# Asking for the next expert's rows late in the turn instead of early

## What is computed

```python
def _moe_swiglu(x, w_router, w_gate, w_up, w_down):
    ...
    logits = (xf @ w_router).astype(jnp.float32)
    top_logit, top_idx = lax.top_k(logits, TOP_K)        # 8 experts, 2 per token
    top_w = jax.nn.softmax(top_logit, axis=-1)
    ...
    def expert_block(args):
        xs, e = args
        return (jax.nn.silu(xs @ w_gate[e]) * (xs @ w_up[e])) @ w_down[e]
    ...
    out = jnp.zeros_like(xf).at[row_token].add(y_rows)   # weighted rows, added at their token
```

## Time and profile before

| | |
|---|---|
| median of three runs | 2572.55 us |
| the profiled execution: its time, its span | 2571.28 us, 2569.5 us |
| PE (TensorE matmuls) busy | 2514.3 us, 98% |
| DVE (VectorE) busy | 1837.9 us, 72% |
| ACT (ScalarE) busy | 1302.9 us, 51% |
| POOL (GpSimd) busy | 125.7 us, 5% |
| granted TensorE clock, mean | 0.993 |
| HBM over the span | 219 GB/s |

### The profile page before, as it was taken

One profiled execution on the slowest core, in us unless ns is written; L12 is line 12 of the kernel. 1 busy time (PEld: TensorE's weight loads), 2 busy tenths in 40 slices (PEclk: granted clock), 3 DMA queues, 4 the chain that ended last, 5 costly groups with the idle time before them and its releaser, 6 DMA issues.

```text
span 2569.5 us, 41311 instructions
## 1 busy us (share of the span) xinstructions
PE 2514.3 (98%) x16342; PEld 2169.7 (84%) x16342; DVE 1837.9 (72%) x2266; ACT 1302.9 (51%) x1535; POOL 125.7 (5%) x136
## 2 busy tenths in 40 slices
PE   8999999999999999999999999999999999999997
PEld 7888999878899988789998887888888888888886
DVE  6657777855777555365555643689899899899898
ACT  5454545553544431224334212267677677777775
POOL 1100000300000001200000111000000000000000
PEclk9999999999999999999999999999999999999999
DMA  5344553423544431136554321399999999999995
GB/s 213 131 181 155 188 196 133 147 99 131 213 179 183 148 131 67 67 131 237 183 178 148 116 68 66 128 377 366 357 370 360 363 367 356 364 368 354 363 369 225
DMA packets 78909, 563.96 MB, mean 219 GB/s; under 512 B 8880, under 2 KB 9136, under 8 KB 11440
## 3 DMA queue, kind: packets, MB, share of 16 engines
q1 hardware_dynamic: 76320, 550.93, 57.2%
q0 software_dynamic: 2448, 11.01, 1.1%
HBM read 559.81 MB, written 2.10 MB: 219 GB/s over the span
## 4 chain that ended last, share of the span: by engine, by line
PE 91%; DVE 4%; ACT 3%; issue 2%; DMA 0%; DVEq 0%; ACTq 0%; SPq 0%; POOL 0%
PE bank L655 24%; PE bank L1141 18%; PE bank L1166 10%; PE bank L645 10%; PE bank L684 7%; PE bank L716 4%; PE bank L736 3%; PE bank L669 2%; DVE w_lo L2503 1%; PE bank L1151 1%; PE bank L963 1%; PE bank L977 1%; PE bank L974 1%; ACT w_hi L1659 1%; PE bank L810 1%
## 5 line engine op out<-in xcount | busy, mean ns | idle before, releaser
L2503 DVE TENSOR_TENSOR w_lo<-ring,w_hi 128x2048 fp32r<-128x2048 f32 x216 | 486.0, 2288 | 46.8 <-ACT w_hi L1659 46.8
L1659 ACT ACTIVATE w_hi<-ring 128x2048 fp32r<-128x2048 f32 x216 | 405.0, 1917 | 20.2 <-PE bank L1141 16.7
L1141 PE MATMUL bank<-w_hi,xe_hi 128*128 128x512 f32 x792 | 312.0, 394 | 1.1
L1141 PE MATMUL bank<-w_lo,xe_hi 128*128 128x512 f32 x792 | 308.8, 390 | 0.0
L1141 PE MATMUL bank<-w_hi,xe_lo 128*128 128x512 f32 x792 | 308.2, 389 | 0.0
L655 PE MATMUL bank<-x_hi,w_hi 128*128 128x256 f32 x1008 | 285.3, 283 | 0.0
L655 PE MATMUL bank<-x_hi,w_lo 128*128 128x256 f32 x1008 | 285.2, 283 | 0.0
L655 PE MATMUL bank<-x_lo,w_hi 128*128 128x256 f32 x1008 | 285.2, 283 | 0.0
L1754 DVE TENSOR_TENSOR w_lo<-ring,w_hi 128x2048 fp32r<-128x2048 f32 x97 | 222.1, 2290 | 86.1 <-ACT w_hi L1280 84.0
L645 PE MATMUL bank<-xT,ring 128*128 128x256 f32 x1088 | 253.8, 385 | 1.1 <-ACT Z L1568 1.1
L1280 ACT ACTIVATE w_hi<-ring 128x2048 fp32r<-128x2048 f32 x99 | 189.4, 1914 | 109.2 <-PE bank L684 71.4
(11 more groups left out here) (378 smaller groups left out, 5093.1 us busy)
## 6 DMA issues: line engine op xcount, KB each, us to landing
ring<-in_stream SPq DMA_DIRECT2D x431, 1024.0 KB, 5.1
yT<-in_stream SPq DMA_DIRECT2D x54, 1024.0 KB, 6.9
xT<-in_stream SPq DMA_DIRECT2D x27, 1024.0 KB, 7.2
Z<-in_stream SPq DMA_DIRECT2D x8, 1024.0 KB, 8.3
norm_rows<-in_rows POOLq DMA_DIRECT2D x4, 1024.0 KB, 7.7
par<-in_par SPq DMA_DIRECT2D x1, 1335.0 KB, 9.7
cst<-in_cst SPq DMA_DIRECT2D x1, 1216.0 KB, 13.6
xres<-in_x SPq DMA_DIRECT2D x2, 512.0 KB, 4.5
```

What stands on the lines that cost most here:

```text
L1141: r = mm(banks[4 + j % 2], a[:, k, :], moe_part(b, i)[:, q * 512:(q + 1) * 512], start=(k == 0 and a is xe_hi and b is w_hi), stop=(k == K ...
L1659: act_(moe_part(w_hi, at), moe_slot(at), ACT.Copy).then_inc(*A.done("moe_hi", at))
L2503: v.tensor_tensor(moe_part(w_lo, at), moe_slot(at), moe_part(w_hi, at).bitcast(F32), ALU.subtract)\
```

## The change

The one-hot matrix for the next turn is made at j = 7 behind that for `pickw` instead of at j = 2. TensorE multiplies it with the token numbers at j = 8, right behind the transposes of `pickw`, instead of at j = 4. VectorE copies `row_at` at j = 9, ahead of `pickT`, instead of at j = 5, and behind the waits for `slot_weight` and the scatter. GpSimd's code is the same; it issues the gather when the copy is done. TensorE's wait for `row_at` ahead of the transposes at j = 8 is gone. No instruction other than that wait is added or removed.

```diff
@@ TensorE, in turn()
                         if j == 8:
-                            pe.wait_ge(*V.of("row_at"))
                             pe.wait_ge(*V.of("pickw"))
                             for tb in range(TB):
                                 r = nc.tensor.transpose(banks[7][:, tb * P:(tb + 1) * P], pickw[:, tb, :], ct("ident"))
                             r.then_inc(*T.done("pickT"))
-                        if j == 4:
                             pe.wait_ge(*V.of("pick"))
                             for tb in range(TB):
                                 r = mm(banks[7][:, 256:257], pick[:, tb, :], ct("token", tb, 1), start=(tb == 0), stop=(tb == TB - 1))
@@ VectorE, in turn()
                                 if not peeled:
                                     ve.wait_ge(*T.before("pickT"))
                                 one_hot(pickw, n, "wgt", "pickw")
-                            if j == 2:
                                 ve.wait_ge(*(T.of("gather0", 1) if peeled else T.before("gather", 1)))
                                 one_hot(pick, n + 1, "sel", "pick")
-                            if j == 5:
-                                ve.wait_ge(*T.of("row_at"))
-                                v.tensor_copy(row_at, banks[7][:, 256:257]).then_inc(*V.done("row_at"))
                             if j == 9:
                                 ve.wait_ge(*A.of("slot_weight"))
                                 ve.wait_ge(*T.of("scattered", 1))
+                                ve.wait_ge(*T.of("row_at"))
+                                v.tensor_copy(row_at, banks[7][:, 256:257]).then_inc(*V.done("row_at"))
                                 v.tensor_scalar(pickT, banks[7][:, 0:256], 0.0, None, ALU.is_gt).then_inc(*V.done("pickT"))
```

## The result

The changed kernel has a median of 2587.32 us over six runs (2581.06 to 2590.23), the kernel before 2572.18 beside them (2571.28 to 2573.39): a ratio of 1.0056, 95% interval 1.0044 to 1.0069. It is 15.1 us slower, outside the range, which ended at 2581. The profiled execution has 2585.63 us for a span of 2583.8, 14.3 us over the span before.

A forecast was written before the change was run, and what follows sets the result against it. PE (TensorE), busy for 98% of the span, was taken as the bound. The terms -0.4 (one restart less) + 0 (DVE) + 0 (waits) + 0.6 (one late gather) = +0.2 us gave a median of 2572.8 us, range 2570.5 to 2581.

The forecast's parts named there:

- What bounds the kernel: Expert stage: PE idles only 0.15 us per 96.90 us turn, so only a new wait of PE could cost much.
- PE's instructions, -0.4 us: Row-number product placed directly behind the weight transposes: one restart instead of two, 9 x -0.05 = -0.4 us.
- DVE, 0: The moved one_hot pair (0.59 us) fits DVE's 0.66 us idle gap and the copy fits another: cost 0.
- The gather, +0.6 us: Gather issued just before PE needs it: of nine landings one, at 8.6 us, would be late by 0.6 us.
- the budget of 7.97: Time from the gather's new issue to PE's need, in us, against a median landing of 7.2: 0.8 to spare.
- The load on the DMA engines: Engine shares near the gather, old place against new: both have an emptier stretch, so the old landing times were kept.
- Rival 1: Gather slow at its new place beside a full weight stream, landing at 8.3 to 8.9 us: +3 to +8.4 us; chance 0.11.
- Rival 2: A running w_lo on DVE delays GpSimd's gather instruction by 2.1 us: 1.3 us per turn, 12 in all, 2584.5; chance 0.08.

The follow-up runs named there:

- late_copy_only: The kernel before with only VectorE's copy of row_at moved to j = 9 and TensorE's wait for row_at gone: 2587.6 us against 2571.68, ratio 1.0057.
- free start: The changed kernel with two more VectorE instructions behind pickT, so the next w_lo starts behind GpSimd's gather instruction: 2575.97 us against 2571.68, ratio 1.0016.
- early_but_held: The kernel before with two more hT_lo instructions ahead of the row_at copy at j = 5, so a w_lo starts first: 2572.59 us, ratio 1.0002.
- half_unit_elsewhere: The changed kernel with only half of weight unit 12 loaded in each turn, 40 us ahead of the gather: 2589.72 us against 2572.01, ratio 1.0069.

## Why the prediction was wrong

- **What bounds the kernel.** Right: PE is the bound, and only a new wait of PE could cost something. (The wait table of before has one more wait of PE than the prediction counts, 3.0 us for y_lo behind the last turn; it plays no part.)
- **PE's instructions, -0.4 us.** Right as far as it can be seen: the order after has one restart (L1195, L1199, then 5.59), and the turns of the kernel with the copy one unit earlier are 0.03 us shorter in the mean. The 0.4 us in all is too small for the runs to show.
- **DVE, 0.** Right: four one_hot take 1.11 us and the next w_lo starts 1.92 us behind the product for the hidden block (2036.93 against 2035.01), where it was 1.93. The weight loads' wait for w_lo is 6.4 us in 16 waits, as before. Late_copy_only, which leaves them where they were, has the same loss.
- **The gather, +0.6 us.** This is the step that failed, at the sentence "I take the nine's own values". The place of the copy, the 0.93 us to the issue and the budget of 7.97 were right. In the turn shown the landing was 2064.07 - 2054.98 = 9.08 us behind the issue, and of the 1.1 us over it PE's matmuls show 0.85 in that turn, since they run 0.23 us behind their weight loads. The latency of 7.2 was read as a property of the gather. It was a property of its place, in two ways: whether a w_lo had started ahead of it on DVE, and how much of the weight stream had been issued ahead of it.
- **The load on the DMA engines.** I compared shares, found an emptier stretch at 2.5 to 5 us behind the issue, and concluded that both places were alike. The emptier stretch is real: with a free start the gather meets it and lands in 5.2 us. The hold-up of 2.06 us lets the next unit go first: it is issued 0.64 us ahead of the end of GpSimd's instruction.
- **Rival 1** (3 to 8 us, a landing up to 8.9) had half of the cause and too low an end: the 8.9 us of a stream unit was no upper bound for a gather that goes behind one.
- **Rival 2** (GpSimd held up by DVE, 12 us, 2584.5) had a chance of 0.08 and came nearest: hold-up 2.1 us predicted, 2.06 measured; a landing 2.1 us later predicted, 1.9 in the median measured; 12 us predicted, 15.1 measured. That it came so near is partly luck. It predicted 1.3 us in every turn; the first six intervals lost 0.04 to 1.04 us, and the last two and the last wait, with late landings and the low clock in one, made up for it. And it added the hold-up to the 7.2 us of the old place, which early_but_held shows to be no rule: there a hold-up of 1.64 us left the landing at 7.0. Here 2.06 us of hold-up and the unit that went ahead by it came on top of the 5.2 us of a free start. The argument against it was empty. That GpSimd's instruction and a w_lo lie over each other without harm in the kernel before says nothing on this case, for there GpSimd had started first in all nine turns. The rule of the Trainium skill, "SBUF — State Buffer", on the two separate sides of SBUF, says that the one that starts first keeps the other out for its whole instruction. The trace agrees for a w_lo that is first (GpSimd's instruction has 3.00 us against 0.94). For a GpSimd instruction that is first it doesn't: the w_lo 0.39 us behind it has its 2.29 us.
- **Chances.** With a budget that only 0.8 us of margin holds up, a hold-up of 2 us and a queue ahead weren't two rivals at 0.08 and 0.11 but the question. Nothing that the prediction read in the trace had measured either.

## What to carry to other kernels

A latency that a trace shows where it is hidden isn't the one to use where it is exposed: ask what was ahead of the transfer on its queues, and what ran on the other engines when it was issued. When a transfer is moved to just ahead of its consumer, give it the margin of at least one unit of the bulk stream (some 2.5 us here) and of one long instruction that can hold its issue (2.3 us here), or leave it early. Here the copy one unit earlier, with 4.1 us more of margin and no hold-up, brought all 15 us back. An instruction whose own duration grows, here from 0.94 to 3.00 us, is the sign of such a hold-up, and its cause is found by looking at which neighbour started first, not at whether they overlap.

## What the runs showed of the hardware

- GpSimd's instruction for an indirect DMA with 128 row numbers seems to begin its work only when a DVE subtraction of two operands in SBUF (the on-chip buffer; 128x2048, float32) that started ahead of it is over. It ends 0.81 to 0.90 us behind the end of that instruction, in all nine turns of each of the six traces in which w_lo was first: 3.00 us where w_lo was 0.10 us ahead, 2.58 where it was 0.53, 2.23 where it was 0.87. A DVE instruction that reads PSUM (128x256) over its first 0.33 us left it at 0.94, and so did a w_lo that started 0.2 to 0.46 us behind it, which kept its own 2.29 us. Which operand of w_lo is the cause wasn't tried.
- The 0.52 MB of the gather landed 5.2 to 10.0 us behind its instruction's start (medians of nine, in the table above). What differs is the hold-up, the weight units issued ahead of the instruction's end, and the stream beside the gather's own packets. The part of the units ahead is shown for one unit by halving it. That the packets go in the order of issue is an inference: it fits the table but for its last row, where they don't keep it strictly.
- Single gathers are 2 to 4 us later than the median (11.3 in the changed kernel, 12.7 in late_copy_only, 8.8 with a free start). In the changed kernel's latest one, all but four packets had gone by 2456.2, and these four took to 2457.8 beside a full stream, for a landing at 2458.3. The stretch between:

```profile
q1 hardware_dynamic: 122, 0.87, 98.1%
q0 software_dynamic: 4, 0.01, 2.2%
```

  In late_copy_only the two latest gathers (11.3 and 12.7 us) had 1.4 and 1.6 MB of the stream ahead of them instead of 1.1. In the changed kernel it was 1.1 and 1.2 MB at the two latest, so that isn't the reason there. Which engine's packets are late, and why in some turns only, is open. Late gathers and the low clock behind them may also be why the changed kernel's runs are spread over 9.2 us against 2.1 before; only one of its executions was traced, so this isn't shown.
- The granted clock fell from 1.00 to 0.50 (1.2 GHz) at PE's wait for the gather of 3.1 us in the changed kernel and at those of eight turns with the copy one unit later (3.3 to 5.8 us), each time for 3.4 or 6.8 us that began within the wait or at most 1.2 us behind its end. It also fell at waits of 2.3, 2.5 and 2.8 us in half_unit_elsewhere and of 3.1 and 4.5 us in late_copy_only. It stayed at 1.00 at the changed kernel's wait of 2.7 us and at all its other waits and those of the other runs of 1.9 us and less. So these waits give no length at which it falls.
